# Five of 17 tiles of the last layer norm scaled and biased by TensorE instead of VectorE

## What is computed

```python
h = layer_norm(alpha * x + mix(x))
f = hier_moe(h)                      # two of 32 experts for every token
y = layer_norm(alpha * h + f, ln2_g, ln2_b)

def layer_norm(x, g, b):
    mu = mean(x);  var = mean(square(x - mu))
    return (x - mu) * rsqrt(var + eps) * g + b
```

## Time and profile before

| | us |
|---|---|
| median of three runs | 1373.07 |
| the three runs | 1369.31, 1373.07, 1374.18 |
| the profiled execution, its own time | 1375.28 |
| its span, first to last instruction | 1373.4 |
| last add of the experts issued | 1311.92 |
| first load of the last part issued | 1318.23 |
| first store issued | 1333.35 |
| last store issued | 1371.06 |

### The profile page before, as it was taken

How to read it: one execution, slowest core, us unless ns; L and a number is a source line. 1 busy time by engine, 2 the same in 40 slices (tenths; PEclk the granted TensorE clock), 3 DMA queues, 4 the chain that set the end, 5 groups by cost and what they waited for, 6 DMA issues and landing times.

```text
span 1373.4 us, 21264 instructions
## 1 busy us (share of the span) xinstructions
PE 1257.1 (92%) x5579; PEld 603.3 (44%) x5580; DVE 740.0 (54%) x2093; ACT 537.3 (39%) x883; POOL 471.0 (34%) x633
## 2 busy tenths in 40 slices
PE   8999997889999998799999999999999999999910
PEld 3444444657666655445555545433333333333300
DVE  2423433463655564748888888544444444444338
ACT  0000001333444443423333332265566666566544
POOL 5113110000000000245555554365565566656321
PEclk9999998999999998999999999999999999999965
DMA  6365554222112166246666554279999999999776
GB/s 254 93 221 158 180 152 157 73 97 69 63 62 77 55 196 186 92 141 216 213 215 219 158 154 124 86 226 318 311 291 368 338 286 332 328 367 362 197 265 262
DMA packets 91256, 273.41 MB, mean 199 GB/s; under 512 B 14888, under 2 KB 41088, under 8 KB 78038
## 3 DMA queue, kind: packets, MB, share of 16 engines
q1 hardware_dynamic: 73975, 226.53, 46.6%
q0 software_dynamic: 14384, 42.32, 12.8%
q10 hardware_dynamic: 2807, 3.53, 0.8%
HBM read 212.80 MB, written 66.40 MB: 203 GB/s over the span
## 4 chain that ended last, share of the span: by engine, by line
PE 46%; issue 30%; DVE 11%; DVEq 5%; DMA 4%; ACT 1%; POOL 1%; POOLq 1%; SPq 1%; ACTq 0%
PE P L1117 13%; PE bank_S L1139 9%; PE M L1117 6%; PE bank_S L737 4%; PE P L737 3%; DVEq L1705 2%; PE bank_T L737 2%; PE M L737 2%; DMA work<-conv_rows 1%; DVE route L1710 1%; PE M L1125 1%; DVE work L1667 1%; PE bank_S L911 1%; DMA big<-sum_rows 1%; ACT work L1429 1%
## 5 line engine op out<-in xcount | busy, mean ns | idle before, releaser
L1379 ACT ACTIVATE big<-big 128x2048 f32 x76 | 145.1, 1910 | 121.8 <-issue 74.6
L1117 PE MATMUL P<-big,work 128*64 x416 | 188.0, 595 | 1.8 <-DVE work L1923 1.5
L1118 PE MATMUL P<-big,work 128*64 128x512 f32 x416 | 188.0, 595 | 0.0
L776 PE MATMUL P<-big,work 128*128 128x256 f32 (+1 forms) x512 | 173.6, 496 | 0.0
L2114 POOL DMA_INDIRECT work<-h_rows,piece_idx x148 | 142.1, 960 | 62.9 <-issue 40.1
L1139 PE MATMUL bank_S<-big,work 128*64 x304 | 136.7, 592 | 1.0 <-DVE work L1907 1.0
L1141 PE MATMUL bank_S<-big,work 128*64 128x512 f32 x304 | 136.7, 592 | 0.0
L2030 POOL TENSOR_SCALAR work<-work 128x1 f32<-128x1 f32 (+1 forms) x17 | 3.8, 222 | 380.0 <-DVE work L1588 380.0
L776 PEld LDWEIGHTS P<-big,work 128*128 128x128 f32 x512 | 97.3, 194 | 70.4 <-issue 63.6
L911 PE MATMUL P<-big,work 128*128 128x512 f32 x256 | 116.4, 608 | 5.0 <-DVE work L1624 5.0
L911 PE MATMUL bank_S<-big,work 128*128 128x512 f32 x256 | 113.8, 597 | 0.0
(11 more groups left out here) (356 smaller groups left out, 2269.4 us busy)
## 6 DMA issues: line engine op xcount, KB each, us to landing
big<-in_w SPq DMA_DIRECT2D x96, 1024.0 KB
work<-in_xt_prompt SPq DMA_DIRECT2D x32, 512.0 KB, 4.3
big<-sum_rows SPq DMA_DIRECT2D x16, 520.0 KB, 8.4
big<-in_toe SPq DMA_DIRECT2D x16, 512.0 KB, 3.3
work<-in_x_prompt SPq DMA_DIRECT2D x16, 512.0 KB, 3.9
h_rows<-work SPq DMA_DIRECT2D x16, 512.0 KB, 2.7
sum_rows<-work SPq DMA_DIRECT2D x16, 512.0 KB, 3.6
out_y_prompt<-big SPq DMA_DIRECT2D x16, 512.0 KB
```

Of the source, the lines that this page charges most:

```text
L776: last = mm(dst[0:n, 0:c1 - c0], lhs[:, k, :], w_qkv[:, k, c0:c1], start=(k == 0), stop=(k == KD - 1))
L1117: mm(lower, xgT[j][:, k, 0:U], both[:, k], start=(k == 0), stop=(k == KD - 1))
L1118: last = mm(upper, xgT[j][:, k, U:P], w_up[:, k], start=(k == 0), stop=(k == KD - 1))
L1379: fn(w_up.rearrange("p k m f -> p m k f")[:, :, ks, :], src, ACT.Copy).then_inc(s[f"wu{part}_ok"], 1)
```

## The change

Five tiles, `SHARED = (2, 5, 8, 11, 14)`, keep their `centred` pass on DVE but lose their `finished` pass. For these:

- ACT makes a 128 x 128 diagonal matrix of the tile's reciprocal roots, `ident * c_rs`, in `sg` or `gs` (`scaled`);
- PE multiplies it with the centred tile and adds the bias by a product of a row of ones with one row of `ln_b`: two products for each half of 512 columns, into `bank_S` or `bank_T` by turns, four in all for a tile;
- ACT copies the 1024 columns from PSUM back to `out_t` (`closed_by_pe`), from where SP stores them.

On ACT `scaled(t)` follows the statistics of tile t + 2, and `closed_by_pe(t)` those of tile t + 5; that of tile 14 comes last of all. SP stores in a new order, `STORED` = 0 1 3 4 2 6 7 5 9 10 8 12 13 11 15 14 16, and waits on `c_act` for the five. Three semaphores of an earlier part of the kernel (`sm_ok`, `s_p`, `sconv_ok`) become one, `sV_ok`, which its three users wait for at the counts 2, 3 and 1, in the order in which DVE raises it.

```diff
+        SHARED = (2, 5, 8, 11, 14)
+        STORED = [t for q in range(0, NT - 1, 3) for t in (q, q + 1, q - 1)[0 if q else 0:3 if q else 2]] + [NT - 1, NT - 2, NT]
+        diag = [sg[:, 0:P], gs[:, 0:P]]
+        closed = [bank_S, bank_T]
...
-            for t in range(NT + 1):
+            for t in STORED:
                 n = rows_of(t)
-                after(sp, s["c_yv"], t)
+                if t in SHARED:
+                    sp.wait_ge(s["c_act"], 2 * SHARED.index(t) + 2)
+                else:
+                    after(sp, s["c_yv"], t - sum(q < t for q in SHARED))
...
+            for q, t in enumerate(SHARED):
+                pe.wait_ge(s["c_act"], 2 * q + 1)
+                after(pe, s["c_ct"], q)
+                for half in range(2):
+                    cols = slice(512 * half, 512 * (half + 1))
+                    mm(closed[q % 2][:, cols], diag[q % 2], out_t[:, t, cols], start=True, stop=False)
+                    last = mm(closed[q % 2][:, cols], C["ones"][0:1, :], ln_b[0:1, cols], start=False, stop=True)
+                last.then_inc(s["c_pe"], 1)
...
+            def scaled(t):
+                act.wait_ge(s["c_rs"], 1 + part_of(t, RSTD))
+                fn(diag[SHARED.index(t) % 2], ident, ACT.Copy, scale=c_rs[:, t:t + 1]).then_inc(s["c_act"], 1)
+
+            def closed_by_pe(t):
+                after(act, s["c_pe"], SHARED.index(t))
+                fn(out_t[:, t, 0:D], closed[SHARED.index(t) % 2][:, :], ACT.Copy).then_inc(s["c_act"], 1)
...
+                if t - 5 in SHARED:
+                    closed_by_pe(t - 5)
+                if t - 2 in SHARED:
+                    scaled(t - 2)
+            closed_by_pe(SHARED[-1])
...
-                stt(zz, zz, c_mv[0:n, t, 0:1], ln_g[0:n, :], ALU.subtract, ALU.mult)
+                last = stt(zz, zz, c_mv[0:n, t, 0:1], ln_g[0:n, :], ALU.subtract, ALU.mult)
+                if t in SHARED:
+                    last.then_inc(s["c_ct"], 1)
...
-                if step >= LAG:
+                if step >= LAG and step - LAG not in SHARED:
                     finished(step - LAG)
```

More of the change, by code:

```diff
@@ L166 @@
 oh_ok pe_rk rk_ev slot_ok sc_out0 sc_out1 last_out s_cache s_row s_vs
-pe_smp sA_ev sm_ok s_p sB_ev sconv_ok
+pe_smp sA_ev sB_ev sV_ok
 early_out tab_build pe_tab eids_ok idx_ok tab_ok tab_in0 tab_in1 tab_in2 tab_in3 tab_in4 tab_in5
@@ L170 @@
 early_li early_ix early_xg early_pe early_act early_ve early_add
-ln2_in c_in0 c_in1 c_in2 c_in3 c_in4 c_in5 c_va c_rs c_yv c_out
+ln2_in c_in0 c_in1 c_in2 c_in3 c_in4 c_in5 c_va c_rs c_yv c_ct c_act c_pe c_out
 """.split()
@@ L354, in layer @@
         LAG = 3
+        SHARED = (2, 5, 8, 11, 14)
+        STORED = [t for q in range(0, NT - 1, 3) for t in (q, q + 1, q - 1)[0 if q else 0:3 if q else 2]] + [NT - 1, NT - 2, NT]
+        assert sorted(STORED) == list(range(NT + 1))
+        diag = [sg[:, 0:P], gs[:, 0:P]]
+        closed = [bank_S, bank_T]
         def part_of(t, parts):
@@ L865, in sample_piece @@
                 elif step == 4:
-                    pe.wait_ge(s["s_p"], 1)
+                    pe.wait_ge(s["sV_ok"], 3)
                     tr(M0[:, 128:192], Ps, ident[0:64, 0:64]).then_inc(s["pe_smp"], 1)
@@ L875, in sample_piece @@
                 elif step == 6:
-                    pe.wait_ge(s["sconv_ok"], 1)
+                    pe.wait_ge(s["sV_ok"], 1)
                     for c in range(CC):
@@ L1220, in sample_piece @@
                 elif step == 3:
-                    act.wait_ge(s["sm_ok"], 1)
+                    act.wait_ge(s["sV_ok"], 2)
                     fn(Ps, M0[0:64, 128:256], ACT.Exp, bias=s_nm, scale=SCALE, accum_out=s_rs)
@@ L1560, in sample_conv @@
                     last = ts(conv_s[:, c, :], conv_s[:, c, :], cw[:, c, TAPS:TAPS + 1], None, ALU.add)
-                last.then_inc(s["sconv_ok"], 1)
+                last.then_inc(s["sV_ok"], 1)
             def sample_max():
@@ L1568, in sample_max @@
                 v.drain()
-                tt(s_dd, s_nm, s_ns, ALU.subtract).then_inc(s["sm_ok"], 1)
+                tt(s_dd, s_nm, s_ns, ALU.subtract).then_inc(s["sV_ok"], 1)
             def sample_norm():
@@ L1576, in sample_norm @@
                 v.drain()
-                ts(Ps, Ps, s_li, None, ALU.mult).then_inc(s["s_p"], 1)
+                ts(Ps, Ps, s_li, None, ALU.mult).then_inc(s["sV_ok"], 1)
             def conv_stats(c):
```

## The result

The changed kernel is **slower** by 0.7%: 1382.09 us median of 15 runs (1377.68 to 1390.31) against 1372.29 (1369.31 to 1378.42, 15 runs) for the kernel before; ratio 1.0068, 95% interval 1.0049 to 1.0088. The forecast was 1368.8 with a range of 1365.2 to 1373.5, so the sign and the range both missed.

A forecast was written before the change was run, and what follows sets the result against it. DVE was taken to bound the last 55 us; removed passes alone would give 6.8 us, but tile 14's chain and the store queue left 4.3, so 1373.07 - 4.3 = 1368.8 us, range 1365.2 to 1373.5.

The forecast's parts named there:

- What bounds the kernel before: Last 55 us: DVE is the bound, starting late at 1327.10 and never catching up, with SP's stores waiting for it.
- What it takes off DVE: Last part: five `finished` passes removed save 6.8 us on DVE, an upper bound of the gain.
- What it adds to ACT: Copy and diagonal cost 1.2 to 1.32 us a pair, moving the end of tile 16's statistics by 3.6 to 4.0.
- What it adds on PE: Each shared tile's four 128x512 products take 3.8 us at the granted clock of 0.50.
- The cover: PE's time hidden before ACT's copy: 2.4 us to spare at tile 2, 1.8 at tiles 5, 8, 11, none at 14.
- The new end: Tile 14's diagonal, products and copy end at 1364.7 to 1365.1; its large store is issued there instead of 1369.7.
- The queue of stores: At the end, four stores within 3 us need until 1367.7, against 1366.9 for tile 14 alone; span ends at 1369.1.
- The estimate that the prediction sets beside this: Last store, by the skill's fixed DMA cost: 2 + 1.25 us from issue to end, an end 0.5 us earlier.
- PE is too slow for its place in ACT's program: Rival: ACT waits for PE ahead of later statistics; at 7.6 us a tile 1379.2 us; chance 0.06.
- DVE still ends it: Rival: tile 14's chain fits under DVE's last passes and stores do not queue; 6.8 us gained, 1366.3; chance 0.18.
- little is left: Rival: tile 14's chain and the store queue are 2 to 3 us worse than forecast; 1371 to 1372; chance 0.18.
- the stores as the bound of the kernel before: Rival: stores, not DVE, bound the end; rejected since 17.2 MB at 420 GB/s are done by 1360; no chance given.

The follow-up runs named there:

- e5: Changed kernel with four shared tiles placed earlier (1, 5, 9, 12), filler products on PE, stores in order 0 to 16; 1370.94 us, ratio 0.9983 to the kernel before.
- e6: Changed kernel with three shared tiles (2, 6, 10), copies six tiles behind, stores as tiles become ready, no fillers; 1369.36 us, ratio 0.9962 to the kernel before.
- e1: Changed kernel with the two bias products of each shared tile left out, so the bias is missing there; 1371.45 us, ratio 0.9992 to the kernel before.
- e7: Changed kernel with its five tiles, copies eight tiles behind, stores as tiles become ready, no fillers; 1377.18 us, ratio 1.0033 to the kernel before.
- e2: Changed kernel plus filler products on PE, four after the expert loop and three after each of the first four shared tiles; 1369.80 us, ratio 0.9980 to the kernel before.

## Why the prediction was wrong, point by point

**What bounds the kernel before: right.** Wherever the shared tiles were nearly covered (e5, e6), fewer passes on DVE shortened the last part, and DVE's passes are the last of the chain again. (The passes that the prediction names f4 and f5 at 1347.37 and 1349.92 are f6 and f7; the pitches read from them hold.)

**What it takes off DVE: right, the upper bound not reached.** In e1 the last pass ends at 1363.74, 47.5 us after the first load, against 52.8 before: 5.3 of the 6.8. The forecast had 46.5 to 47.0.

**What it adds to ACT: right.** At tile 2 the copy began at 1335.87 and the next statistics at 1337.08, 1.21 us for the pair, in the 1.2 to 1.32 of the sum. The copy took 1.02 us and the diagonal 0.39, at the upper of its two bounds, 0.2 and 0.4.

**What it adds on PE: wrong, and this is the step that failed.** "Four 128x512 products after a pause took 3.78 us" read a row's count as a count of products. The row is x4 instructions. The program has eight products in a row at L911 and 256 in all (16 tiles, 2 halves, 8 slices of the contraction), and the trace has twice as many rows there:

```profile
L911 PE MATMUL P<-big,work x256: 592/592/1221, 580.6 to 837.4; 128*128 128x512 f32 x128
L911 PE MATMUL bank_S<-big,work x256: 592/592/697, 601.2 to 854.0; 128*128 128x512 f32 x128
```

(duration ns min/median/max; 512 rows for 256 products). The second row says the same: x8 in 3.60 us, where the program stands at four products of `bank_S<-big,work`. So four products at 0.50 are eight rows, some 7.3 us at the 0.91 us of rows of like products; by turns with the one-row products a row takes 1.0, and the tile 8.05. The term of the sum was 3.8. The clock of 0.50 was as forecast. The Trainium skill has a rule that would have caught it: "FP8 and Floating Point Precision", section "TensorE Precision Notes", says that a true FP32 product takes four passes through the array. By that, four products of 512 columns at 1.2 GHz are an estimated 4 x 4 x 512 / 1.2 = 6827 ns, or 6.8 us; the trace has 8.05, or the 7.3 worked out above for like products, and agrees with four passes and not with the 3.4 of two.

**The cover: right in its size, wrong for this price.** The prediction had 2.4 us of cover at tile 2 and 1.8 at the next three. With 8.05 us a tile the waits come out as 1.9 and 2.5; measured were 2.05, 2.60, 2.30 and 2.60.

**The new end.** The last copy was to end 46.7 us after the first load and ended at 60.8 (1374.83). Of the 14.1 us, 9.5 are those four waits and 4.3 tile 14's own products; 0.3 are left over. From its store to the end I had 3.4 us and measured 3.6.

**The queue of stores: there, and somewhat undersized.** In e1 the price on PE was the one that I had assumed, and the gain was 2.6, not 4.3. About half of the missing part is DVE, which ends 0.5 to 1.0 us later than forecast and waits 1.2 us for ACT's statistics, where 0.7 to 0.8 were expected. ACT's own added work is not the reason: from tile 7 on it is 3.9 us, inside the forecast's 3.6 to 4.0. But the load of tile 7 landed 18.7 us after the first load was issued, against 18.0 in the kernel before and 17.8 in the changed one; that is likely scatter. The rest lies behind DVE. DMA in e1 from 1357 to 1369, in 40 slices of 0.3 us:

```profile
GB/s 423 341 0 0 0 0 0 164 410 396 437 341 0 0 0 0 355 423 410 410 369 410 396 396 396 410 382 423 423 396 423 423 410 205 55 14 0 0 0 0
```

From slice 17 to 34, 1361.8 to about 1367.1, the four stores run without a gap: the 5 us of the sum. The engines are idle for the four slices before, in which tile 11 was ready and stood behind tile 13. The span ends 1.7 to 1.9 us after the last byte where I had 1.4. (The estimate that the prediction sets beside this, 2 + 1.25 us behind the issue at 1364.9, gives 1368.2, 0.9 before 1369.1 and not 0.5; nothing was added up from it.)

**The rivals.** "PE is too slow for its place in ACT's program" is what happened, mechanism and all: I had worked it out for 7.6 us a tile and got 1379.2, with the deciding point at 6.4. The median came 2.9 above that, since a tile cost 8.05. It had a chance of 0.06, since its "against" was the misread row. A rival whose only counter-argument is one row is worth a second look at that row. "DVE still ends it", "little is left" and the stores as the bound of the kernel before did not occur.

## What to carry to other kernels

Before a row of the trace is used as a price, hold its count against the count in the program: here one fp32 product of the code is two PE rows, and at a granted clock of 0.50 they took 2.0 us, where one row in full flow at 1.00 is 0.43 (eight in 3.60, the last of them 0.59). Work that is handed to an idle engine costs nothing only as long as it fits between its input and the place where the program of another engine waits for it, and as long as its sum fits as well (e7); three tiles with copies six tiles behind gained 0.4%, five tiles with copies five behind lost 0.7%. A part at the end of a program is best measured from its own start, since what lies ahead of it moved by up to 9 us from one execution to the next.

## What the runs showed of the hardware that I had not expected

- A product with a single row of ones costs as much as one with 128 rows (2.00 to 2.02 us each in the chain of the changed kernel), and where the two kinds alternate both are slower: 1.00 us an instruction at a granted clock of 0.50 against 0.91 in a row of like products (3 starts in 3.78 less the last one's 1.06), and 0.53 against 0.46 at 1.00 (1.05 for two, 2.77 for six). Whether the single row or the change of weights does it, no run shows.
- Alternating full and one-row products never raised the granted clock from 0.50 here, however busy PE was: not in the changed kernel, busy 11.20 of 14 us, and not in e7, busy 39.00 of 39. Full products alone did: the granted clock rose behind the eight instructions of fillers in e2, and during the last of tile 2's four in e1. Once at 1.00 it stayed there through the alternating products in e2, and in e5 it fell during those of tile 5, behind an idle stretch of 1.58 us. In e1 it stayed at 0.50 for tiles 5 to 14, with 3.78 us of full products and 3.0 to 3.3 of idle time between them. Whether the single row is what keeps the clock down is not shown; no run has 40 us of full products without a gap in the last part.
- Fillers cost little here: e2 put 32 extra instructions on PE, and at tile 14 the diagonal was written at 1359.06 and the first product began at 1359.24, behind the last filler.
